# An attention and state-space stage rewritten: scores in pairs, decay sums brought by DMA, softmax's inverse applied last

## The chip, the cores and the metric

The kernel runs on one core of a Trainium2 chip. The core has a matrix engine (PE, with PEld for its weight loads), three engines for elementwise work (DVE, ACT, POOL), a queue engine for transfers (SP) and an accumulator memory, PSUM, of 8 banks with 512 float32 columns each. The metric is the time on the device in microseconds (us); less is better.

## The reference, cut to what matters

One encoder layer over two sequences of 256 and 512 tokens: a joint input projection, attention and a state-space mixer side by side, an output projection with a layer norm, a mixture of 16 experts, a last layer norm. Batch is 1 and the width 1024. The changed stage computes this:

```python
# attention: 8 query heads and 2 key heads of 64, in blocks of 128 queries
sc = jnp.einsum("bqkgd,bskd->bkgqs", q_blk * hd ** -0.5, k)
pr = jax.nn.softmax(sc, axis=-1)
o  = jnp.einsum("bkgqs,bskd->bqkgd", pr, v)
# state space: chunks of 128 tokens, 2 groups of 4 heads, a forward and a backward scan
seg = a_cum[..., :, None] - a_cum[..., None, :]
decay_in = jnp.exp(jnp.where(lower, seg, -jnp.inf))
cb = jnp.einsum("bclgn,bcsgn->bgcls", cc, bc)
y_diag = jnp.einsum("bgcls,bgrcls,bcsgrp->bclgrp", cb, decay_in, x)     # x = xs * dt
y_off  = jnp.einsum("bclgn,cbgrpn,bgrcl->bclgrp", cc, prev, jnp.exp(a_cum))
y = y_fwd + y_bwd + d_skip * xs          # then times silu(z), and a norm by group
```

## The kernel before, in words

The 768 tokens are 6 tiles of 128 (`NT = 6`): tiles 0 and 1 are the first sequence, 2 to 5 the second. Each engine runs its own program, written out in order, and semaphores connect them; so the order of the code is the order of the work, and a waiting instruction holds everything behind it on its engine.

The stages are: layer norm and the projections of q, k, v, z, x, B and C; the states that enter each chunk (`chunk_state`, PE with DVE and POOL) while q and k are turned so that the head dimension lies on the partitions (`qk_turn`); then the loop of attention and state space; then the output projection `out_proj`, a per-layer gate, the router and the experts, whose weights SP streams in.

The loop goes over 48 attention units (a tile and a head) and 12 state-space groups (a tile and one of 2 groups), four units to a group, that is 12 turns. In a unit PE computes the scores of 128 queries against all 256 or 512 keys (`scores`, L1642, full float32 with k padded by zeros for the other key head), DVE takes their maximum (`row_max`, L1209), ACT the exponential with its sum (L858), DVE the reciprocal, POOL or ACT divides (`normalise`, L620, or L892), PE turns the 2 or 4 blocks (`turn`, L1656), DVE copies them out (`pt_out`, L1218), and for four units together PE multiplies by the values (`pv`, L1665). For a state-space group PE makes the running sums of the decays in PSUM by 16 products of the steps with a triangular matrix (`decay`, L1680), ACT subtracts and takes the exponential (`decays`, L871 and L875), PE makes the product of C and B (`cb`, L1690), DVE weights the decays with it (`weights`, L1241), POOL adds the two directions (L628), and PE multiplies by x (`y`, L1707). The part that enters from outside the chunk is `before` on PE (L1699). PSUM banks: scores 0 to 2, turned probabilities 3, values 4, sums 5 and 6, `cb` and `y` 7.

What sets the order around the loop: PE waits for all turned q and k and all states ahead of it; SP issues the loads of the output projection's weights behind the last input projection (`load_wout(2, 0)`) and behind the last `before`; the output projection waits for the last attention output, the last y, and the split of its weights into a high and a low half by ACT and DVE. The experts' first weight loads wait for the output projection (`s_o`), the next for the gate (`s_pg`).

## Time and profile before

| quantity | value |
|---|---|
| median of 3 runs | 1155.25 us (1151.55 to 1155.29) |
| the profiled execution's own time | 1152.7 us |
| its span | 1150.9 us |
| mean granted clock of PE | 0.977 |
| busy share of PE / DVE / ACT / POOL | 91% / 38% / 22% / 22% |

Busy shares are averages over stages that have different limits, so the stage of interest has to be looked at by itself. In the traces a matmul in full float32 shows as two records, one in the single-pass format (operands rounded to it, fp32r) as one; their durations overlap, and what a matmul costs in a stream is the distance from one start to the next. "128*32" in a row of PE means weights with 128 rows and 32 columns. A timeline row merges neighbours of one kind: its second number is their joint duration, with the last one's end.

### The profile page before, as it was taken

The page shows a single profiled execution, that of the slowest core. Times are in us where ns is not written, and L with a number is a line of the kernel's source. Part 1 is how long each engine was busy: PE and PEld are TensorE (multiplying, and loading weights), DVE is VectorE, ACT ScalarE, POOL GpSimd, SP SyncE. Part 2 cuts the span into 40 slices and gives each one's busy share as a digit, 9 for nine tenths or more (in the row PEclk, how much of TensorE's full clock was granted, in tenths as well). Part 3 has the DMA queues.
Part 4 walks back from the last instruction along what each step waited for, and adds up shares of the span by engine and source line. Part 5 has one row for each costly group of instructions (what it writes and reads, how often), then busy time and mean ns, then how long its engine had stood idle before and what let it go on. Part 6 is the DMA issues. An engine that isn't in the chain of part 4 may idle for free.

```text
span 1150.9 us, 18483 instructions
## 1 busy us (share of the span) xinstructions
PE 1051.5 (91%) x7713; PEld 562.8 (49%) x7713; DVE 434.2 (38%) x834; ACT 258.2 (22%) x548; POOL 250.9 (22%) x295
## 2 busy tenths in 40 slices
PE   5999787978999899898999999999999999999990
PEld 3568666655555587765643333333333333333330
DVE  5426786356777877757200111101001110010117
ACT  1143244266656631230010000000000000000004
POOL 0005995224455200000100111011111110111110
PEclk9999989989999999999999999999999999999995
DMA  9110200110000351403259999999999999999976
GB/s 329 31 42 32 74 1 1 41 70 0 1 1 1 95 189 72 184 20 128 97 215 406 388 389 406 391 390 402 388 387 390 399 395 390 395 397 388 403 269 232
DMA packets 60810, 253.96 MB, mean 221 GB/s; under 512 B 7127, under 2 KB 11095, under 8 KB 44382
## 3 DMA queue, kind: packets, MB, share of 16 engines
q1 hardware_dynamic: 52542, 234.48, 52.0%
q0 software_dynamic: 8224, 18.88, 6.4%
q8 instruction: 29, 0.48, 0.2%
q14 instruction: 15, 0.12, 0.0%
HBM read 237.62 MB, written 15.73 MB: 220 GB/s over the span
## 4 chain that ended last, share of the span: by engine, by line
PE 68%; DVE 12%; DMA 8%; POOL 6%; ACT 3%; issue 2%; SPq 0%; DVEq 0%; POOLq 0%; ACTq 0%
PE ps L1918 25%; PE ps L1927 12%; DMA ring<-in_w_e_up 5%; PE ps L1559 4%; PE ps L1665 2%; PE ps L1680 2%; PE ps L1553 2%; DMA late<-in_w_e_up 2%; PE ps L1813 1%; PE ps L1770 1%; PE ps L1771 1%; PE ps L1772 1%; PE ps L1798 1%; PE ps L1799 1%; PE ps L1800 1%
## 5 line engine op out<-in xcount | busy, mean ns | idle before, releaser
L1918 PE MATMUL ps<-late,mix 128*32 128x512 f32 x1536 | 171.1, 593 | 0.7 <-DMA late<-in_w_e_up 0.7
L1918 PE MATMUL ps<-ring,mix 128*32 128x512 f32 x1536 | 170.7, 592 | 0.9 <-DMA ring<-in_w_e_up 0.8
L1441 DVE TENSOR_TENSOR mix<-mix,ps 128x768 f32<-128x768 f32 x16 | 15.3, 954 | 324.2 <-ACT mix L1002 324.2
L1002 ACT ACTIVATE mix<-ps 128x768 f32<-128x768 f32 x16 | 13.0, 810 | 479.0 <-PE ps L1918 479.0
L1918 PEld LDWEIGHTS ps<-ring,mix 128*32 128x32 f32 x1536 | 49.7, 110 | 116.4 <-issue 112.5
L1918 PEld LDWEIGHTS ps<-late,mix 128*32 128x32 f32 x1536 | 48.1, 110 | 109.8 <-issue 107.4
L1927 PE MATMUL ps<-late,mix 128*32 128x256 f32 (+1 forms) x1024 | 86.0, 487 | 1.3 <-issue 1.3
L1927 PE MATMUL ps<-ring,mix 128*32 128x256 f32 (+1 forms) x1024 | 85.7, 486 | 0.9 <-DMA ring<-in_w_e_down 0.9
L1448 DVE TENSOR_SCALAR mix<-ps,att 128x256 f32<-128x256 f32 (+1 forms) x30 | 17.1, 614 | 143.0 <-PE ps L1927 143.0
L1927 PEld LDWEIGHTS ps<-ring,mix 128*32 128x32 f32 x1024 | 33.1, 110 | 50.0 <-issue 37.8
L690 POOL COPY idx_now<-idxT 96x1 int32 (+1 forms) x14 | 2.5, 180 | 244.3 <-PE ps L1896 244.3
L1927 PEld LDWEIGHTS ps<-late,mix 128*32 128x32 f32 x1024 | 31.9, 110 | 43.7 <-issue 31.5
L685 POOL DMA_INDIRECT acc_rows<-mix,idx_now x30 | 46.8, 1561 | 15.0 <-POOL idx_now L693 10.5
L1533 PE MATMUL ps<-xl,wh 128*128 128x512 f32 (+1 forms) x128 | 45.1, 353 | 0.0
L1559 PE MATMUL ps<-ring,xT 128*128 128x512 f32 x96 | 43.9, 612 | 1.2 <-ACT xT L734 1.2
L1642 PE MATMUL ps<-xT 128*128 128x512 f32 (+1 forms) x96 | 43.6, 539 | 1.3 <-issue 1.3
L693 POOL COPY idx_now<-idx 128x2 int32 (+1 forms) x16 | 3.0, 185 | 190.2 <-DVE mix L1448 186.9
L1798 PE MATMUL ps<-ring_r,xT_r 128*128 128x512 f32 x96 | 40.5, 422 | 1.6 <-DVE cst L1379 1.6
L858 ACT ACTIVATE ring<-ps,att 128x512 f32<-128x512 f32 (+1 forms) x48 | 29.3, 611 | 48.8 <-DVE att L1210 48.7
L1119 DVE SCALAR_TENSOR_TENSOR late<-late,cw 128x770 f32<-128x770 f32 x32 | 39.1, 1226 | 0.8
L1656 PE MATMUL ps<-cst,ring 128*128 128x128 f32 x160 | 27.3, 286 | 11.9 <-DVE late L1218 5.5
L1799 PE MATMUL ps<-late_r,xT_r 128*128 128x512 f32 x96 | 37.5, 390 | 0.0
(298 smaller groups left out, 1779.2 us busy)
## 6 DMA issues: line engine op xcount, KB each, us to landing
late<-in_w_e_gate SPq DMA_DIRECT2D x32, 1024.0 KB, 18.6
late<-in_w_e_up SPq DMA_DIRECT2D x32, 1024.0 KB, 20.6
ring<-in_w_e_gate SPq DMA_DIRECT2D x32, 1024.0 KB, 16.8
ring<-in_w_e_up SPq DMA_DIRECT2D x32, 1024.0 KB, 20.6
late<-in_w_e_down SPq DMA_DIRECT2D x16, 2048.0 KB, 22.4
ring<-in_w_e_down SPq DMA_DIRECT2D x16, 2048.0 KB, 22.4
ring<-in_w_in SPq DMA_DIRECT2D x3, 2048.0 KB, 8.9
late<-in_w_ple_gate SPq DMA_DIRECT2D x2, 2048.0 KB, 15.0
```

The costliest lines, as they stand in the source:

```text
L685: pool.indirect_dma_start(acc_parts[i], bass.IndirectOffsetOnAxis(ap=idx_now[:, 1 + i:2 + i], axis=0), ye[i], None, compute_op=ALU.add).th ...
L858: nc.scalar.activation(prob[:, u % 4, 0:L], ps[:, u % 3, 0:L], ACT.Exp, bias=att[:, 0, u:u + 1], scale=HD ** -0.5, accum_out=att[:, 1, u:u ...
L1119: ins = nc.vector.scalar_tensor_tensor(conv[:, m, :], u_pad[:, m, j:j + CW], cw[:, m, j:j + 1], conv[:, m, :], ALU.mult, ALU.add)
L1533: nc.tensor.matmul(o, w_h, xl[:, k, a * P:(a + w) * P], start=False, stop=False)
L1553: last = nc.tensor.matmul(bank[:, 0:272], lhs[k], wkv[:, k, :], start=(k == 0), stop=(k == KD - 1))
L1559: last = nc.tensor.matmul(bank, lhs[k], slotk[0][:, k, :], start=(k == 0), stop=(k == KD - 1))
L1642: nc.tensor.matmul(ps[:, u % 3, 0:n * P], qT[:, h % 4, t * P:(t + 1) * P], kz[:, h // 4, a * P:(a + n) * P], start=True, stop=True).then_i ...
L1656: last = nc.tensor.transpose(ps[:, 3, b * P:(b + 1) * P], prob[:, u % 4, b * P:(b + 1) * P], ident)
L1798: nc.tensor.matmul(o, x_h, wpg_h[h][:, k, :], start=(k == 0), stop=False)
L1799: nc.tensor.matmul(o, x_h, wpg_l[h][:, k, :], start=False, stop=False)
L1918: last = nc.tensor.matmul(ps[32 * j:32 * (j + 1), GU + g, :].rearrange("p (w c) -> p w c", w=2), xeT[:, k, 32 * g:32 * (g + 1)], gu_w[q][: ...
L1927: last = nc.tensor.matmul(ps[32 * j:32 * (j + 1), DN + i, 0:cols], src[:, k, 32 * g:32 * (g + 1)], w[:, cols * c:cols * (c + 1)], start=(k ...
```

## The change

The loop now goes over 24 pairs of units; a pair is one head of each key head. Scores are three single-pass products of high and low halves of q and k (`qh`, `ql`, `kh`, `kl`), each over 64 contraction rows for one of the two key heads, into two neighbouring banks. The maximum is taken for a pair at once. Probabilities are turned undivided; ACT copies them out, not DVE; the values are multiplied pair by pair into 64 partitions for each key head; and the inverse of the sums is spread over the output's shape by PE once a tile (`inverse_rows`), copied by ACT, and multiplied in as the output is copied. The running sums of the decays aren't made anew by PE: they are turned once, written to DRAM, and SP brings them back spread over all partitions, 512 KB for each group (`load_cum`), into two buffers. DVE subtracts and clips them with the logarithm of dt added (`exponents`), ACT takes one exponential for all, and POOL multiplies with C·B (`decayed`), which PE makes for all groups ahead of the loop. The carried part and y now share bank 6; banks 0 to 3 hold scores, 4 and 5 what is turned, 7 the values.

The diff is cut to its core; many of the removed lines are in the functions above.

```diff
-        att_units = [(t, 4 * i + j) for t in range(NT) for i in range(NKV) for j in range(4)]
+        att_units = [(t, i, j) for t in range(NT) for j in range(4) for i in range(NKV)]
         NU = len(att_units)
-        NG = NU // 4
+        NPAIR = NU // 2
+        NG = NT * GROUPS
...
+        def score_bank(p):
+            return 2 * (p % 2)
+        def turn_slot(u):
+            return u + u // 8
+        def slot_free(k):
+            t, i = (k - 2) // 9, (k - 2) % 9
+            return (s_rbc, t + 1) if i == 8 else (s_pts, 8 * t + i + 1)
...
+            sp.wait_ge(s_cro, 1)
+            sp.dma_start(cum_rows, cum_out).then_inc(s_crd, 16)
+            cum_units = cum_rows.rearrange("(t d g h) l -> t g d (h l)", t=NT, d=2, g=GROUPS)
+            def load_cum(n):
+                t, g = ssd_units[n]
+                sp.dma_start(decs[n % 2].rearrange("p d h l -> p d (h l)"),
+                             bc(cum_units[t, g])).then_inc(s_decl[n % 2], 16)
+            sp.wait_ge(s_crd, 16)
             sp.wait_ge(s_proj, len(groups))
+            load_cum(0)
             load_wout(2, 0)
+            sp.wait_ge(s_st, len(upd))
+            load_cum(1)
+            for n in range(2, NG):
+                sp.wait_ge(s_m, n - 1)
+                load_cum(n)
+            sp.wait_ge(s_sc, NU)
...
+            def decayed(n):
+                dec = decs[n % 2]
+                pool.wait_ge(s_edec, n + 1)
+                pool.wait_ge(s_cbs, n + 1)
+                ch.step(nc.gpsimd.tensor_tensor(dec, dec, cbT.unsqueeze(2).broadcast_to([P, 2, HPG, P]),
+                                                ALU.mult))
+                ch.settle()
+                if n >= 2:
+                    pool.wait_ge(s_y, n - 1)
+                nc.gpsimd.tensor_tensor(msums[n % 2], dec[:, 0], dec[:, 1], ALU.add).then_inc(s_m, 1)
...
+            for n in range(NG):
+                decayed(n)
+                if n:
+                    gate(n - 1)
+                ssd_sums(n)
+            gate(NG - 1)
...
+            def cb_out(m):
+                act.wait_ge(s_cb, m + 1)
+                if m == 0:
+                    act.wait_ge(s_conv, KC)
+                copy(cbs[:, 4 * m:4 * m + 4, :],
+                     ps[:, 4 + m % 2, :].rearrange("p (n l) -> p n l", l=P)).then_inc(s_cbc, 1)
...
+            def pt_out(u):
+                t, i, j = att_units[u]
+                n = seq_of[t][1]
+                act.wait_ge(s_pt, u + 1)
+                if u >= 8:
+                    act.wait_ge(s_pv, u // 2 - 3)
+                copy(probT(u)[:, 0:n, :],
+                     ps[:, 4 + turn_slot(u) % 2, 0:n * P].rearrange("p (b c) -> p b c", c=P)).then_inc(s_pts, 1)
+            def inverse_rows_out(t):
+                act.wait_ge(s_rb, t + 1)
+                if t:
+                    act.wait_ge(s_ao, t)
+                copy(inv_rows, ps[:, 4 + (9 * t + 8) % 2, :]).then_inc(s_rbc, 1)
+            def decays(n):
+                act.wait_ge(s_dsc, n + 1)
+                v = decs[n % 2].rearrange("p d h l -> p (d h l)")
+                nc.scalar.activation(v, v, ACT.Exp).then_inc(s_edec, 1)
...
+            for p in range(NPAIR + 1):
+                if p < NPAIR:
+                    probabilities(2 * p)
+                    probabilities(2 * p + 1)
+                if p % 4 == 1 and p >= 5:
+                    inverse_rows_out((p - 5) // 4)
+                if p:
+                    pt_out(2 * p - 2)
+                    pt_out(2 * p - 1)
+                if p % 2 == 0 and p < NPAIR:
+                    decays(p // 2)
+                if p % 2 and p >= 5:
+                    squares((p - 5) // 2)
...
+            def qk_low(t):
+                dve.wait_ge(s_qkh, t + 1)
+                b = 2 * ((U_QK + t) % 2)
+                tc = slice(t * P, (t + 1) * P)
+                nc.vector.scalar_tensor_tensor(ql(t), ps[:, b, :], HD ** -0.5, qh[:, t, :], ALU.mult, ALU.subtract)
+                nc.vector.tensor_tensor(kl[:, tc], ps[:, b + 1, 0:P], kh[:, tc], ALU.subtract).then_inc(s_qkT, 1)
...
+            def row_max(p):
+                L = seq_of[att_units[2 * p][0]][1] * P
+                b = score_bank(p)
+                dve.wait_ge(s_sc, 2 * p + 2)
+                nc.vector.reduce_max(att[:, 0, 2 * p:2 * p + 2], ps[:, b:b + 2, 0:L], X,
+                                     negate=True).then_inc(s_max, 1)
+            def inverse_sums(t):
+                dve.wait_ge(s_exp, 8 * t + 8)
+                nc.vector.reciprocal(att[:, 2, 8 * t:8 * t + 8], att[:, 1, 8 * t:8 * t + 8]).then_inc(s_rcp, 1)
+            def att_out(t):
+                dve.wait_ge(s_pv, 4 * t + 4)
+                dve.wait_ge(s_rbc, t + 1)
+                nc.vector.tensor_tensor(mix[:, t, 0:512], ps[:, 7, :], inv_rows, ALU.mult).then_inc(s_ao, 1)
...
+            def exponents(n):
                 t, g = ssd_units[n]
...
+                dve.wait_ge(s_decl[n % 2], 16 * (n // 2 + 1))
                 for d in range(2):
                     for h in range(HPG):
                         c = d * NH + g * HPG + h
...
+                        v = decs[n % 2][:, d, h]
+                        last = nc.vector.tensor_scalar(v, v, d16(CSUB)[:, t, c:c + 1], d16(LDT)[:, t, c:c + 1],
+                                                       ALU.add, ALU.min)
+                last.then_inc(s_dsc, 1)
...
+            for p in range(NPAIR + 2):
+                if p < NPAIR:
+                    row_max(p)
+                if p % 4 == 0 and p:
+                    inverse_sums(p // 4 - 1)
+                if p % 2 and p < NPAIR:
+                    carried(p // 2)
+                if p % 2 == 0 and p >= 4:
+                    y_out(p // 2 - 2)
+                if p % 2 == 0 and p < NPAIR:
+                    exponents(p // 2)
+                if p % 4 == 1 and p >= 5:
+                    att_out((p - 5) // 4)
...
-            def scores(u):
-                t, h = att_units[u]
+            def scores(p):
+                t, _, j = att_units[2 * p]
                 a, n = seq_of[t]
-                if u >= 3:
-                    pe.wait_ge(s_exp, u - 2)
-                nc.tensor.matmul(ps[:, u % 3, 0:n * P], qT[:, h % 4, t * P:(t + 1) * P],
-                                 kz[:, h // 4, a * P:(a + n) * P], start=True, stop=True).then_inc(s_sc, 1)
+                if p >= 2:
+                    pe.wait_ge(s_exp, 2 * p - 2)
+                b = score_bank(p)
+                jc = slice(j * P, (j + 1) * P)
+                for step, (q, k) in enumerate(((qh[:, t, jc], kh), (qh[:, t, jc], kl), (ql(t)[:, jc], kh))):
+                    for i in range(NKV):
+                        rows = slice(i * HD, (i + 1) * HD)
+                        last = nc.tensor.matmul(ps[:, b + i, 0:n * P], q[rows], k[rows, a * P:(a + n) * P],
+                                                start=(step == 0), stop=(step == 2))
+                        if step == 2:
+                            last.then_inc(s_sc, 1)
...
+            def pv(p):
+                t, _, j = att_units[2 * p]
+                a, n = seq_of[t]
+                pe.wait_ge(s_pts, 2 * p + 2)
+                if j == 0 and t:
+                    pe.wait_ge(s_ao, t)
                 for b in range(n):
...
+                    for i in range(NKV):
+                        rows = slice(i * HD, (i + 1) * HD)
+                        last = nc.tensor.matmul(ps[rows, 7, j * P:(j + 1) * P],
+                                                kvd[:, a + b, P + i * HD:P + (i + 1) * HD],
+                                                probT(2 * p + i)[:, b, :], start=(b == 0), stop=(b == n - 1))
                 last.then_inc(s_pv, 1)
...
+            def inverse_rows(t):
+                k = 9 * t + 8
+                pe.wait_ge(s_rcp, t + 1)
+                pe.wait_ge(*slot_free(k))
+                for j in range(4):
+                    for i in range(NKV):
+                        u = 8 * t + 2 * j + i
+                        last = nc.tensor.matmul(ps[i * HD:(i + 1) * HD, 4 + k % 2, j * P:(j + 1) * P],
+                                                att[:, 2, u:u + 1].broadcast_to([P, HD]), ident,
+                                                start=True, stop=True)
+                last.then_inc(s_rb, 1)
...
             def y(n):
                 t, g = ssd_units[n]
                 pe.wait_ge(s_m, n + 1)
+                pe.wait_ge(s_offm, min(n + 2, NG))
+                if n:
+                    pe.wait_ge(s_yo, n)
...
+            for p in range(NPAIR + 2):
+                if p < NPAIR:
+                    scores(p)
+                if p >= 2:
+                    pv(p - 2)
+                if p % 4 == 1 and p >= 5:
+                    inverse_rows((p - 5) // 4)
+                if 1 <= p <= NPAIR:
+                    turn(2 * p - 2)
+                    turn(2 * p - 1)
+                if p % 2 == 0 and p < NPAIR:
+                    before(p // 2)
+                if p % 2 and p >= 3:
+                    y((p - 3) // 2)
```

On PE, a piece of the loop before, in the long turns (`xT` holds q and k, `ring` the probabilities and states, `late` here x, B and C, `gb_in` turned probabilities, `kvd` the values); 16 decay products of 128x128 stand ahead of it and behind it:

```order
L1656 MATMUL ps<-cst,ring 128x128 x4
L1642 MATMUL ps<-xT 128x512
L1690 MATMUL ps<-late 128x128
L1656 MATMUL ps<-cst,ring 128x128 x4
L1642 MATMUL ps<-xT 128x512
L1656 MATMUL ps<-cst,ring 128x128 x4
L1699 MATMUL ps<-ring,late 128x256 x2
L1665 MATMUL ps<-gb_in,kvd 128x512 x4
L1642 MATMUL ps<-xT 128x512
L1707 MATMUL ps<-late,ring 128x64 x4
```

And the like piece of the changed kernel, two pairs:

```order
L1758 MATMUL ps<-gb_in,kvd 64x128 x8
L1745 MATMUL ps<-cst,ring 128x128 x8
L1784 MATMUL ps<-ring,late 128x256
L1733 MATMUL ps<-kh,qh 128x512 x2
L1733 MATMUL ps<-kl,qh 128x512 x2
L1733 MATMUL ps<-kh,ql_53 128x512 x2
L1758 MATMUL ps<-gb_in,kvd 64x128 x8
L1770 MATMUL ps<-cst,att 64x128 x8
L1745 MATMUL ps<-cst,ring 128x128 x8
L1795 MATMUL ps<-late 128x64 x4
```

The decay products and C·B are gone from the loop; scores, values and the spread inverse are in small tiles, between turns and y in full ones.

On DVE, before, one unit's rows and the state-space part of a turn:

```order
L1209 TENSOR_REDUCE att<-ps 128x1
L1210 TENSOR_SCALAR att<-att 128x1
L1311 RECIPROCAL att<-att 128x1
L1218 COPY late<-ps 128x4x128
L1233 TENSOR_TENSOR late<-ps,cst 128x256
L1241 SCALAR_TENSOR_TENSOR ring<-ring,dtw,late 128x128 x8
L1252 TENSOR_TENSOR ring<-ps,dtw 128x256 x2
```

And in the changed kernel, a pair and the state-space part that follows it:

```order
L1281 TENSOR_REDUCE att<-ps 128x2
L1317 TENSOR_TENSOR ring<-ps,dtw 128x256 x2
L1281 TENSOR_REDUCE att<-ps 128x2
L1286 RECIPROCAL att<-att 128x8
L1327 TENSOR_TENSOR late<-late,ps 128x256
L1300 TENSOR_SCALAR ring<-ring,dtw 128x128 x8
L1305 TENSOR_TENSOR late<-late,cst 128x256
```

The y sum (L1327), which releases POOL's gate and sums, now stands right ahead of the eight scalars and the mask.

## Rows read from the trace of the kernel before

**Rows 1.** the table of windows: us from A to B, busy of each engine, PEclk, DMA share, GB/s.

```profile
281.00:388.00 107.00, 98.35 (x475) 62.04 (x476) 81.74 (x233) 66.10 (x177) 53.77 (x53) 1.00 0.01 3
596.00:1150.00 554.00, 522.09 (x5276) 185.35 (x5268) 68.31 (x106) 38.86 (x73) 68.92 (x76) 0.98 1.00 380
```

**Rows 2.** timeline of PE, turn from 333 to 347 us: start, us, line, operation, count.

```profile
333.40 1.00 PE L1707 MATMUL ps<-late,ring 128*128 128x64 f32 x8
334.21 1.98 PE L1680 MATMUL ps<-tri_r,a_r 128*128 128x128 f32 x16
336.04 0.62 PE L1656 MATMUL ps<-cst,ring 128*128 128x128 f32 x4
336.49 1.02 PE L1642 MATMUL ps<-xT 128*128 128x512 f32 x2
341.86 1.03 PE L1699 MATMUL ps<-ring,late 128*128 128x256 f32 x4
342.73 3.60 PE L1665 MATMUL ps<-gb_in,kvd 128*128 128x512 f32 x8
347.02 1.00 PE L1707 MATMUL ps<-late,ring 128*128 128x64 f32 x8
```

**Rows 3.** timeline of PE: where the loop, its long turns, its end and the next stage start.

```profile
235.14 0.67 PE L1642 MATMUL ps<-xT 128*128 128x256 f32 x2 [1.34 <-issue]
281.76 1.98 PE L1680 MATMUL ps<-tri_r,a_r 128*128 128x128 f32 x16
388.45 1.00 PE L1707 MATMUL ps<-late,ring 128*128 128x64 f32 x8
398.68 0.50 PE L1770 MATMUL ps<-ring_r,xT_r 128*128 128x512 f32 x1 [0.35 <-DVE mix L1224]
```

**Rows 4.** instructions by source line: duration ns min/median/max, first and last start, forms.

```profile
L1209 DVE TENSOR_REDUCE att<-ps x48: 404/678/694, 235.9 to 388.1; 128x1 f32<-128x512 f32 x32, 128x1 f32<-128x256 f32 x16
L1241 DVE SCALAR_TENSOR_TENSOR ring<-ring,dtw,late x96: 343/347/353, 241.6 to 386.2; 128x128 f32<-128x128 f32 x96
L1054 DVE TENSOR_SCALAR xa<-xa,mv,sd x12: 811/812/815, 6.3 to 479.9; 128x1024 f32<-128x1024 f32 x12
L858 ACT ACTIVATE ring<-ps,att x48: 455/679/689, 236.5 to 389.0; 128x512 f32<-128x512 f32 x32, 128x256 f32<-128x256 f32 x16
L628 POOL TENSOR_TENSOR ring<-ring x12: 1261/1262/1269, 243.9 to 386.6; 128x512 f32<-128x512 f32 x12
L636 POOL TENSOR_TENSOR late<-late,ring x16: 722/724/732, 245.8 to 388.7; 128x256 f32<-128x256 f32 x16
```

**Rows 5.** timeline of POOL and DVE from 386.6 us.

```profile
386.62 1.27 POOL L628 TENSOR_TENSOR ring<-ring 128x512 f32<-128x512 f32 x1 [3.49 <-DVE ring L1241]
386.78 1.39 DVE L1277 SCALAR_TENSOR_TENSOR mix<-mix,gss,ssdw 128x256 f32<-128x256 f32 x1
389.53 0.47 DVE L1277 SCALAR_TENSOR_TENSOR mix<-mix,gss,ssdw 128x256 f32<-128x256 f32 x1
```

**Rows 6.** table of windows of 5 us: PEclk is the granted clock.

```profile
240.00:245.00 5.00, 1.49 (x6) 0.80 (x6) 3.69 (x16) 2.64 (x9) 1.09 (x1) 0.94 0.00 0
245.00:250.00 5.00, 4.78 (x23) 4.78 (x23) 0.63 (x4) 1.24 (x5) 2.37 (x4) 0.50 0.00 0
365.00:370.00 5.00, 3.50 (x16) 1.92 (x16) 4.93 (x14) 3.45 (x10) 2.46 (x2) 1.00 0.01 3
405.00:410.00 5.00, 5.00 (x23) 4.13 (x22) 5.00 (x6) 2.49 (x5) 0.00 (x0) 1.00 1.04 403
```

**Rows 7.** timeline of PE in the expert stage, one change of product.

```profile
699.62 1.04 PE L1918 MATMUL ps<-ring,mix 128*32 128x512 f32 x8
700.59 1.13 PE L1896 MATMUL ps<-cst,mix 96*128 96x96 f32 x8
701.65 5.37 PE L1927 MATMUL ps<-late,mix 128*32 128x256 f32 x64
```

**Rows 8.** DMA issues by tile: count, KB each, median us from issue to landing.

```profile
gb_in<-in_ln_in_g SPq DMA_DIRECT2D x1, 512.0 KB, 5.7
```

More of the change, by code:

```diff
@@ L846, in _ @@
                 b = 2 * (u % 2)
[L847 to L851 removed]
+                nc.scalar.activation(qh[:, t, :], ps[:, b, :], ACT.Copy, scale=HD ** -0.5)
+                copy(kh[:, t * P:(t + 1) * P], ps[:, b + 1, 0:P]).then_inc(s_qkh, 1)
@@ L1221, in att_out @@
[L1221 to L1236 removed]
+                if n > len(upd) // 2 and n % 2:
+                    qk_low((n - len(upd) // 2) // 2)
@@ L1620, in _, with cb @@
                         chunk_state(n)
+            def cb(m):
+                pe.wait_ge(s_projo, len(groups))
+                if m == 2:
+                    pe.wait_ge(s_cbc, 1)
+                for n in range(4 * m, 4 * m + 4):
+                    t, g = ssd_units[n]
+                    cc = conv_col(t)
+                    last = nc.tensor.matmul(ps[:, 4 + m % 2, (n % 4) * P:(n % 4 + 1) * P], conv[:, 4 + g, cc:cc + P],
+                                            conv[:, 6 + g, cc:cc + P], start=True, stop=True)
+                last.then_inc(s_cb, 1)
             def qk_turn(t):
@@ L1686, in cb, with before @@
+            def before(n):
                 t, g = ssd_units[n]
```

314 lines of the change are left out of this document (107 added, 207 removed).

## The prediction

> **What bounds the kernel now.** I read three views in this order: the table of windows, to find the stage that the change rewrites and what is busy in it; the timeline of PE through that stage, to get the length of one turn of its loop; the groups by source line, for the price of one operation on each engine. In the windows [rows 1] the reader is to see that from 281 to 388 us PE is busy 98.35 of 107 us while DVE has 81.7, ACT 66.1 and POOL 53.8: this stage goes by PE. In the last window the DMA queues have share 1.00 for 554 us: the experts stream their weights at full rate, and that stream starts when the stages before it are done. Its first loads wait for the output projection and its other ones for the gates, so whatever the attention stage saves arrives earlier at the same stream and is kept one for one.
>
> The loop has 12 turns, one for each token tile and state-space group, with 4 heads' attention in each. Turns 0 to 3 belong to the sequence of 256 tokens, 4 to 11 to that of 512. PE's first scores start at 235.14, the long turns at 281.76, and the last y product at 388.45 [rows 3]: 153.3 us, 11.7 for a short turn (46.6 / 4) and 13.3 for a long one (106.7 / 8). One long turn in full [rows 2] runs from 333.40 to 347.02, 13.6 us. PE's part of it: y 0.81; decays 1.83; four groups of turned probabilities at 0.46, 1.83; four scores, each two records of 0.43, 3.44; two state products 0.87; values 3.43; C·B 0.4. That is 12.6, so waits take about 0.8.
>
> **The change, part by part, for a long turn.** Durations are from one profiled execution of 1152.7 us (span 1150.9 plus 1.8 around it); the median of the timed runs is 1155.25, from 1151.55 to 1155.29.
>
> PE loses the 16 decay matmuls (1.83; DMA now spreads the sums in time) and the C·B product (0.4, made ahead of the loop). Turns, state products and y stay: 1.83 + 0.87 + 0.81 = 3.5. Scores become 12 single-pass matmuls over half the contraction rows. PE does 23 of the full-width kind in 5 us [rows 6], 0.22 each: 2.6 one after another, 1.3 if the two halves of the rows run side by side. Values become 16 products with 64 output partitions and 128 columns, two records each; a record of a quarter of 0.43 is 0.107, so 3.4 in sequence and 1.7 if the two halves of the output partitions go together. The spread inverse costs 8 such records for a turn, 0.9 or 0.45. The trace shows no half tiles. It shows quarter ones: 8 records of an expert product with 32 weight columns lie within 0.97 us [rows 7], though one of 512 columns in full width takes 0.43. So I take side by side for both, and the sequence as the other bound.
>
> PE changes the shape of its tile some 6.5 times in a turn. The nearest rows are the expert's transposes between tiled products: 8 of them take 1.06 us from their start to the next product's start [rows 7], where 8 at the 0.11 of [rows 2] would take 0.9. That is some 0.07 for one change. The other bound is what a group of four transposes lasts (0.62) beyond its spacing (0.45) [rows 2], 0.17, if each shape waits for the last one to be through. I take 0.15, nearer to that, since in the loop each group is short: 1.0 us. Sum for PE: 3.5 + 1.3 + 1.7 + 0.45 + 1.0 = 8.0; in sequence 3.5 + 2.6 + 3.4 + 0.9 + 1.0 = 11.4. The Trainium skill ("TensorEngine Tiling (Array Packing)", Key Properties) says that changing the tiling mode drains TensorE and that different tiles may run in parallel; the rows agree with the second for columns, and no row shows it for contraction rows.
>
> DVE loses the copies of turned probabilities, the negation and single reciprocals. Its maximum goes over two banks at once: 678 ns for 512 columns and 404 for 256 [rows 4] give 1.07 ns a column, so 1.23, twice, 2.5. Eight weighted products (347 ns each, 2.2 for all eight) become eight two-operation scalars of 128 columns; 1024 columns of such an instruction take 812 ns [rows 4], so 128 lie between 0.15 and the 0.27 of today's spacing; 0.2, so 1.6. With C·B masked 0.4, carried part 0.75, y sum 0.4, half an output 0.34: 6.0. ACT: four exponentials with their sums at 0.68 spacing (2.7), four copies out at a little less each (2.5, from DVE), one exponential of 1024 columns for the decays (679 ns for 512 and 455 for 256 [rows 4], so 1.1), half an inverse copy 0.3, squares 0.5: 7.1; before it had eight small activations more. POOL gives up its normalising (1.5 each) and takes the product with C·B: 1.26 for 512 and 0.72 for 256 [rows 4] is 2.1 ns a column, 2.34 for 1024; then 1.26, 0.6, 1.5, 0.7: 6.4.
>
> So no engine alone has over 8 us. But DVE and POOL get in each other's way. At 386.78 a DVE product of two SBUF operands takes 1.39 us, beside a POOL sum that began at 386.62 and ended at 387.89 [rows 5]; the same instruction 2.7 us later takes 0.47 us. It was held till POOL was done. In today's loop POOL mostly waits for DVE's eight products, so they don't meet; in the new one POOL's gate and sums are released by the y sum right ahead of DVE's eight scalars. If these and the mask never run beside a POOL instruction, the two need 6.4 + 1.6 + 0.4 = 8.4 together, and behind the eight scalars stand the next maximum and all that follows it. I take 10.0 for a long turn: 8.4, and 1.6 for waits between four engines that are all near it (twice the 0.8 of today). A short turn has one carried sum fewer: 7.7, with waits 8.7; PE has 5 there. The Trainium skill ("SBUF — State Buffer", Who interferes with whom) says that DVE in a two-port mode, or with two SBUF inputs, and GpSimd block each other for a whole instruction, and that tensor_scalar has such a mode. That rule speaks against this change; the row agrees for two SBUF inputs. With it the turn is 10.0, without it 8.8.
>
> Sum of the loop: 4 x 8.7 + 8 x 10.0 = 115, against 153.3: 38 less.
>
> Ahead of the loop PE gets 12 C·B products (about 3 us, some of it in its waits), and DVE the low halves of q and k, 6 x (0.67 + 0.28) = 5.7 (the 0.67 and 0.28 by the prices of PSUM reads in [rows 4]), in a stretch in which it steps with PE. Bounds 0 and 9, all hidden or none; I take 4. The new loads of the sums, 512 KB each, land in about 6 us, as the row of that size says [rows 8]. A buffer's circle is load 6, eight scalars 1.6, ACT 3, POOL 3.6, so 14 for two turns: hidden under 2 x 8.7. From landings of 9 or 10 on it shows.
>
> The tail from the last scores to the first output projection at 398.68 [rows 3] has the same members (values, y, copies, weight halves): 0, bounds -3 and +3. 1152.7 - 38 + 4 = 1118.7, so **1119**; the median stands 0.2% over the profiled run, which I leave in the range.
>
> **Rivals.** (A) DVE and POOL hardly meet, and PE sets the pace with half tiles in parallel: 8.0 + 0.8 a long turn, 7 a short one: 98, so 1152.7 - 55 + 4 = 1102. For it: each engine's own work is under 8. Against: the row at 386.78.
>
> (B) The halves do not overlap on PE: 11.4 + 0.8 = 12.2 a long turn, 8.7 a short one: 132, so 1152.7 - 21 + 4 = 1136. For it: no row shows contraction halves together. Against: the quarter tiles.
>
> (C) Slower: PE, no longer full, is given the lower clock. At 240 to 245 us PE is busy 1.49 of 5 us, and from 245 to 250 its granted clock is 0.50, 1.2 GHz for 2.4 [rows 6]. The streaming parts then double: 15.0 + 0.8 long, 10 short: 166, +13 and +4: 1170. It decides when this clock holds for about two thirds of the loop: 115 + 51 x 0.67 = 149, which with the 4 ahead is 153. Against: from 365 to 370, with PE busy 3.50 of 5, it keeps 1.00 [rows 6].
>
> (D) The change doesn't carry: the loads of the sums or a handshake through bank 6, which the carried part and y now share, hold each turn at today's length: 153 + 4, so 1157 at most, and about 1150 if short turns gain. Bank 6 makes y wait for DVE's carried part of the next turn, which stands behind a maximum; PE has turned probabilities to do meanwhile (0.9 + 1.7 against 1.2 + 0.75), so I expect under 0.5.
>
> **How the numbers follow.** Forecast 0.48 (1108 to 1129), A 0.20, B 0.20, C 0.06, D 0.06. Below 1096 lies 0.06 of A, above 1144 all of C and D and 0.02 of B: range 1096 to 1144. A measurement of this kernel tells 0.5% (6 us) from no change. Faster: all of the forecast, A and B, 0.88. C is slower; D ends within 0.5% with 0.04 and beyond with 0.02: same 0.04, slower 0.08.
>
> **What would show it.** Right: PE's first scores near 239, its share of the loop down to some 80%, turns of 10 and 8.7 us; single scalars on DVE stretched to over 1 us where a POOL instruction runs; score records of two halves starting within 0.05 us of each other in pairs. Wrong: pairs 0.22 apart (B); scalars all at 0.15 to 0.3 (A); a granted clock of 0.50 over most windows of the loop (C); PE or DVE waiting for the DMA of the sums, or long waits before y (D). A last window that isn't as long as today's 554 us would break the step that the gain is kept.

## The result, and the profile after

The changed kernel takes 1137.81 us (median of 4 runs, 1137.32 to 1143.67) beside 1155.27 for the kernel before: ratio 0.9868, 95% interval 0.9848 to 0.9888. The forecast was 1119. The move of 17.5 us has the forecast sign, but is half of the 36 that were forecast. The profiled run took 1138.14, span 1135.6.

The engines' row of the page after, and its windows (in front of the loop, the loop, the experts); the columns are those of [rows 1]:

```profile
PE 1021.4 (90%) x7906; PEld 555.2 (49%) x7906; DVE 414.1 (36%) x678; ACT 241.2 (21%) x468; POOL 247.1 (22%) x283
```

```profile
core 0: us, PE busy (x) PEld busy (x) DVE busy (x) ACT busy (x) POOL busy (x), PEclk, DMA share, GB/s
225.00:245.00 20.00, 12.59 (x75) 10.29 (x73) 12.38 (x31) 7.74 (x17) 2.08 (x3) 0.84 0.60 157
245.00:375.00 130.00, 106.06 (x856) 81.00 (x856) 91.41 (x183) 76.76 (x191) 71.10 (x64) 0.84 0.21 66
580.00:1135.00 555.00, 521.70 (x5272) 185.09 (x5261) 68.30 (x106) 38.85 (x73) 68.73 (x76) 0.98 0.99 379
```

PE is no longer full in the loop (82% of 130 us, where [rows 1] had 92%), no other engine is either, and the granted clock is 0.84. The experts' window, moved ahead with the stream, holds the same work (PE busy 521.7 us where [rows 1] had 522.1) and still runs at the rate of the DMA: what is saved ahead of it arrives.

The marks of [rows 3], looked up in the timeline of PE after, give the whole balance:

| part | before | after | difference | forecast |
|---|---|---|---|---|
| start to first scores | 235.14 | 244.92 | +9.8 | +4 |
| first scores to last y | 153.3 | 127.0 | -26.3 | -38 |
| last y to end of span | 762.4 | 763.7 | +1.2 | 0 |
| span | 1150.9 | 1135.6 | -15.3 | -34 |

Two steps failed: the loop by 12 us and the lead-in by 6. The first shows in PE's timeline of one and a half long turns (start, time from first start to last end, operation; in brackets the idle time ahead of it and what ended it), the stretch that answers to [rows 2]:

```profile
335.81 0.50 PE L1733 MATMUL ps<-kh,qh 64*128 64x512 f32 x2
336.14 0.40 PE L1733 MATMUL ps<-kl,qh 64*128 64x512 f32 x2
336.38 0.40 PE L1733 MATMUL ps<-kh,ql 64*128 64x512 f32 x2
336.70 1.09 PE L1758 MATMUL ps<-late,kvd 128*64 128x128 f32 x16
337.73 1.09 PE L1745 MATMUL ps<-cst,ring 128*128 128x128 f32 x8
339.52 1.08 PE L1795 MATMUL ps<-late,ring 128*128 128x64 f32 x8 [0.70 <-issue]
...
345.29 1.09 PE L1758 MATMUL ps<-gb_in,kvd 128*64 128x128 f32 x16 [0.41 <-ACT gb_in L781]
346.22 1.04 PE L1770 MATMUL ps<-cst,att 128*64 128x128 f32 x16
347.19 0.65 PE L1745 MATMUL ps<-cst,ring 128*128 128x128 f32 x4
350.71 0.63 PE L1745 MATMUL ps<-cst,ring 128*128 128x128 f32 x4 [2.87 <-ACT qksq L781]
351.18 1.22 PE L1795 MATMUL ps<-late 128*128 128x64 f32 x6
```

The spread of the inverse sums (L1770) is done at 347.2, and the second group of turned probabilities needs its bank. That bank comes free only when ACT has copied the spread, and ACT's timeline shows what stands ahead of that copy:

```profile
347.09 1.06 ACT L935 ACTIVATE ring<-ring 128x1024 f32<-128x1024 f32 x1 [1.85 <-DVE ring L1300]
348.64 0.69 ACT L914 ACTIVATE ring<-ps,att 128x512 f32<-128x512 f32 x1 [0.48 <-DVE att L1281]
...
349.31 0.68 ACT L914 ACTIVATE ring<-ps,att 128x512 f32<-128x512 f32 x1
...
349.98 0.59 ACT L781 ACTIVATE qksq<-ps 128x512 f32<-128x512 f32 x1
```

The decays, then both exponentials of the new pair, then the copy. The list of waits in the loop adds these up, and says what else the engines wait for (us in total, times, longest):

```profile
DVE att L1281 <- PE ps L1733: 24.6, 11, 3.7
...
PE ps L1745 <- ACT qksq L781: 12.5, 5, 2.9
...
ACT ring L935 <- DVE ring L1300: 10.3, 6, 2.5
ACT late L935 <- DVE late L1300: 10.3, 6, 3.0
```

12.5 us in five waits. Behind the last four of them the granted clock is lower: 0.66, 0.70, 0.57 and 0.64 in the windows of 5 us from 285, 305, 330 and 350, with 1.00 from 335 to 340 between. Behind the first, at 266.9, it stays at 1.00. The lower clock also comes without such a wait: 0.50 from 365 to 370, behind waits of only 0.66 and 1.00. At the lower of the two levels (1.2 GHz for 2.4) the 16 value products at 331.70 last 1.97 us, those at 336.70 last 1.09.

A second wait stands ahead of y in each turn without a spread, and it is the handshake through bank 6. The profile calls most of it "issue", which means that it saw no releaser:

```profile
PE ps L1795 <- issue: 5.0, 5, 2.1
...
PE ps L1795 <- DVE ring L1317: 1.3, 1, 1.3
```

By the code y waits for POOL's sum of its own group, for DVE's last y sum, and for DVE's carried part (L1317) of the next group. For the y at 339.52, shown above, these two rows tell which came last:

```profile
327.52 1.27 POOL L673 TENSOR_TENSOR ring<-ring 128x512 f32<-128x512 f32 x1
...
338.68 0.74 DVE L1317 TENSOR_TENSOR ring<-ps,dtw 128x256 f32<-128x256 f32 x2
```

POOL was done at 328.79, DVE's y sum at 333.40, the carried part at 339.42, 0.1 us before y starts. All six waits, 6.3 us together, end 0.10 to 0.14 us behind the carried part, which stands on DVE behind the eight scalars, the mask and a maximum.

The collision of DVE and POOL that the prediction feared is there. DVE and POOL, the same stretch; the eight scalars (L1300) take 3.98 us beside POOL's gate and sums (3.4 to 4.0 over the long turns):

```profile
319.66 0.37 DVE L1327 TENSOR_TENSOR late<-late,ps 128x256 f32<-128x256 f32 x1
319.95 3.98 DVE L1300 TENSOR_SCALAR ring<-ring,dtw 128x128 f32<-128x128 f32 x8
```

```profile
320.11 0.76 POOL L693 TENSOR_TENSOR mix<-late,mix 128x256 f32<-128x256 f32 x1 [1.09 <-DVE late L1327]
320.83 0.61 POOL L681 TENSOR_TENSOR late<-late,hpar 128x256 f32<-128x256 f32 x1
321.52 1.55 POOL L684 TENSOR_TENSOR late<-late,ring 128x256 f32<-128x256 f32 x2
```

At 246.68, with POOL idle, the same eight take 2.13. Beside three POOL instructions of 256 columns, as at 298.58, they take 3.42, beside four 3.98: each costs the scalars 0.4 to 0.5 us, less than the 0.6 to 0.8 that it lasts. A single scalar lasts at most 0.90 us there; one of 1.88 stands in the group of 250.59, which takes 5.62 beside POOL's product with C·B.

Ahead of the loop DVE makes a low half (L1250) between two state updates and waits for a q that ACT hasn't copied; PE's state products (L1679) then wait for DVE. First DVE, then PE:

```profile
230.53 0.69 DVE L1250 SCALAR_TENSOR_TENSOR ql<-ps,qh 128x512 fp32r<-128x512 f32 x1 [2.56 <-ACT kh L781]
...
235.24 0.69 DVE L1250 SCALAR_TENSOR_TENSOR ql<-ps,qh 128x512 fp32r<-128x512 f32 x1 [1.91 <-ACT kh L781]
```

```profile
232.35 0.67 PE L1679 MATMUL ps<-qksq,late 128*128 128x256 f32 x2 [2.16 <-DVE ring L1270]
237.06 0.67 PE L1679 MATMUL ps<-qksq,late 128*128 128x256 f32 x2 [2.17 <-DVE ring L1270]
...
244.92 0.58 PE L1733 MATMUL ps<-kh,qh 64*128 64x256 f32 x2 [1.82 <-issue]
```

### The profile page after: what moved, and what is told of

Its sections match the earlier page's. It is cut to its first block, busy times and chain, and to the rows that moved or that the text cites. A ratio compares the mean times of both kernels' runs of the same rounds, so it can differ in the third digit from the quotient of the medians.

```text
span 1135.6 us, 18623 instructions
## 1 busy us (share of the span) xinstructions
PE 1021.4 (90%) x7906; PEld 555.2 (49%) x7906; DVE 414.1 (36%) x678; ACT 241.2 (21%) x468; POOL 247.1 (22%) x283
## 4 chain that ended last, share of the span: by engine, by line
PE 67%; DVE 13%; DMA 8%; POOL 5%; ACT 3%; issue 3%; SPq 0%; ACTq 0%; DVEq 0%; POOLq 0%
PE ps L2003 25%; PE ps L2012 12%; DMA ring<-in_w_e_up 5%; PE ps L1626 4%; PE ps L1620 2%; DVE ring L1300 2%; DMA late<-in_w_e_up 2%; PE ps L1854 2%; PE ps L1897 2%; DVE late L1178 1%; PE ps L1856 1%; PE ps L1855 1%; PE ps L1733 1%; PE ps L1882 1%; PE ps L1883 1%
## 5 line engine op out<-in xcount | busy, mean ns | idle before, releaser
L1508 DVE TENSOR_TENSOR mix<-mix,ps 128x768 f32<-128x768 f32 x16 | 15.3, 954 | 324.2 <-ACT mix L1061 324.2
L1745 PE MATMUL ps<-cst,ring 128*128 128x128 f32 x160 | 27.8, 316 | 12.5 <-ACT qksq L781 12.5
L1884 PE MATMUL ps<-ring_r,mix_r 128*128 128x512 f32 x96 | 37.4, 390 | 0.0
```

The lines of the kernel that those rows point to most:

```text
L1745: last = nc.tensor.transpose(ps[:, 4 + k % 2, b * P:(b + 1) * P], prob[:, u % 4, b * P:(b + 1) * P], ident)
L1884: nc.tensor.matmul(o, x_l, wpg_h[h][:, k, :], start=False, stop=False)
```

## The experiments

"Loop" below is first scores to last y in the profiled run, 127.0 for the changed kernel. The kernels e1 to e4 and e8, e11 are the changed kernel with one edit; e5 has two edits; e6 and e7 stand on e5, e9, e10 and e12 on e6. Loops, clocks and waits are each read from one profiled execution; the timed runs of one kernel lie up to 9 us apart, so a loop is told from another only to a few us.

**e1: the inverse's copy ahead of the exponentials.**

```
 for p in range(NPAIR + 1):              # ScalarE
+    if p % 4 == 1 and p >= 5:
+        inverse_rows_out((p - 5) // 4)
     if p < NPAIR:
         probabilities(2 * p); probabilities(2 * p + 1)
-    if p % 4 == 1 and p >= 5:
-        inverse_rows_out((p - 5) // 4)
```

> ScalarE copies the rows of the inverse sums before the two exponentials of the new pair, and not behind them, twice in the loop of pairs (and once where no exponentials follow). Theory (the copy's place costs TensorE three waits of 2.1 to 2.9 us and, with them, the full clock for the rest of each turn): the waits at 266.9, 327.5 and 350.7 of the trace after shrink to under 1 us, the mean granted clock of the loop rises from 0.84 to 0.90 or more, and the time falls by 6 to 12 us against the changed kernel, to 1126 to 1132. Rival (the exponentials come later by the copy, and the next pair's scores, whose banks they free, wait as long): the time moves by under 3 us, 1135 to 1141, and the waits turn up before the scores.

Measured: 1125.83 (1122.70 to 1126.50), ratio 0.9739, 0.9723 to 0.9755. 12.0 us less than the changed kernel, the theory's upper end; loop 112.3; clock 0.91. The copy moves in five turns, not in two as the expectation says, and two of the five waits stay at 1.2 us, above the 1 that was expected. In the list of waits of e1 the row is now:

```profile
PE ps L1745 <- ACT qksq L781: 4.4, 5, 1.2
```

One reordering on an engine that is 59% busy is worth two thirds of what the whole change had brought. The waits ahead of y stay, 8.1 us in five, and behind the one of 1.84 us at 329.81 the clock falls to 0.66 here too.

**e2: the scalars ahead of y.**

```
 # VectorE, even p
+exponents(p // 2)
 if p >= 4: y_out(p // 2 - 2)
-exponents(p // 2)
```

> VectorE makes the eight scalar products of the exponents before it gates y, so that they don't run beside GpSimd's gate. Theory (the two engines hinder one another: eight took 3.98 us beside GpSimd and 2.13 alone, and ScalarE's decay waits for them): the eight take 2.2 us or less in every even turn, the even turns get shorter by 1 to 1.8 us each, and the time falls by 6 to 12 us, to 1126 to 1132. Rival (the gate of y then runs beside GpSimd's other tiles and is late by as much, or GpSimd's are not what the turn ends on): the scalars get shorter, the turns don't, and the time stays within 3 us of 1137.8.

Measured: 1144.36 (1143.37 to 1145.09), ratio 0.9901, 0.9886 to 0.9917: 6.5 us more. The scalars did come down to 2.1, but y sums up in bank 6, which PE wants for the next product with the states; those now wait for it:

```profile
DVE att L1281 <- PE ps L1733: 44.9, 20, 3.7
...
PE ps L1784 <- DVE late L1327: 22.8, 10, 3.3
```

Both theories failed: a new wait, of 22.8 us, took the place of the collision. In the order as it stands the shared bank costs the 6.3 us of waits ahead of y and none of these; here it is the other way round (0.7 ahead of y for DVE).

**e3: low halves a slot later.**

```
-if n > len(upd) // 2 and n % 2:         # VectorE
-    qk_low((n - len(upd) // 2) // 2)
+if n > len(upd) // 2 + 2 and n % 2:
+    qk_low((n - len(upd) // 2) // 2 - 1)
-if t == 0: cb_out(2)                    # ScalarE
+if t == 1: cb_out(2)
```

> Ahead of the loop VectorE takes each low half of q one slot later, and ScalarE takes the third bank of cb after the second q and not after the first. Theory (the 7.6 us that the lead-in gained between 225 and 245 come of VectorE standing at a low half for a q that ScalarE has not yet, so that the states' products, and TensorE behind them, wait 2.16 us twice): the first scores start at 240 or 241 instead of 244.9, and the time falls by 4 to 6 us, to 1132 to 1134. Rival (the last low halves, now after the states, hold the first scores back by as much): first scores at 244 to 246, the time within 2 us of 1137.8.

Measured: 1131.51 (1129.69 to 1134.15), ratio 0.9799, 0.9782 to 0.9817; 6.3 us less, just over the 4 to 6 that were expected. First scores at 240.36, DVE's waits of 2.56 and 1.91 are gone and so are PE's of 2.16. The theory holds: over the profiled executions the first scores start at 243.1 to 246.6 in the six kernels without this edit and at 239.7 to 241.2 in the seven with it.

**e4: one half after the other.**

```
-for step, (q, k) in enumerate(...):     # scores
-    for i in range(NKV):
+for i in range(NKV):
+    for step, (q, k) in enumerate(...):
-for b in range(n):                      # values
-    for i in range(NKV):
+for i in range(NKV):
+    for b in range(n):
```

> The scores' and values' products of the two halves of the rows are written one half after the other instead of in turns; nothing else is changed. Theory (the products of the two halves run side by side when they alternate, as their steps of 0.23 to 0.24 us for two of 512 columns say): each long turn costs TensorE 0.6 to 0.7 us more in the scores and about 0.9 us more in the values, 11.4 against 8.0 at most, so 1 to 3 us more for each of eight pairs, 1148 to 1162. Rival (the halves already run one after the other, the records only overlap; case B of the prediction): no change, 1136 to 1140.

Measured: 1137.27 (1131.98 to 1140.98), ratio 0.9832, 0.9812 to 0.9853: no more than the changed kernel. By the time alone the rival would have won. The timeline of PE says otherwise:

```profile
337.54 0.51 PE L1733 MATMUL ps<-kh,qh 64*128 64x512 f32 x2
337.87 0.40 PE L1733 MATMUL ps<-kl,qh 64*128 64x512 f32 x2
338.10 0.41 PE L1733 MATMUL ps<-kh,ql 64*128 64x512 f32 x2
338.44 1.58 PE L1758 MATMUL ps<-late,kvd 128*64 128x128 f32 x16
339.95 1.09 PE L1745 MATMUL ps<-cst,ring 128*128 128x128 f32 x8
```

The scores still start in pairs of the two halves, 0.23 apart, though three of the one half are now written ahead of three of the other; two of 512 columns in the time that one full-width product takes ([rows 6]). PE took them out of the order in which they were written. The values, eight of a half behind each other, take 1.51 to the next start in place of 1.03. So the halves do run side by side; PE lost 0.5 us in a pair of heads and the time did not rise. A part went into PE's waits, those ahead of y fell from 6.3 to 3.2 us, and the clock was 0.88 for 0.84; how much each gave isn't parted.

**e5: e1 and e3 together** (both edits above).

> The two edits that each won time, together: the inverse's copy ahead of the exponentials, and the low halves of q a slot later. Theory (the one removes waits inside the loop of pairs, the other waits ahead of it, and nothing links them): the gains of 12.0 and 6.3 us add up, 1119.5, with the first scores at 240.4 and the first output product some 119 us later at 359.7. Rival (the tail takes part of it back, for example a transfer of weights that would be late now): over 1123.

Measured: 1121.29 (1119.13 to 1126.27), ratio 0.9709, 0.9695 to 0.9722. Of the 18.3 us 16.5 are there; with runs from 1119 to 1126 they add up, and this is the forecast's 1119 within 0.2%. First scores (239.7 for 239) and loop (114.8 for 115) are the forecast's too, but partly by luck: the loop still holds 9.8 us of waits ahead of y, which the prediction put at under 0.5 each.

**e6: e5, and y ahead of the maximum.**

```
+if p % 2 == 0 and p >= 4:               # VectorE
+    y_out(p // 2 - 2)
 if p < NPAIR:
     row_max(p)
 ...
-if p % 2 == 0 and p >= 4:
-    y_out(p // 2 - 2)
```

> The two edits of the run before, and VectorE adds y up (the bank's read) before it takes the row maxima of the new pair, so that GpSimd's gate and sums start a maximum earlier and VectorE's eight scalars begin when GpSimd is nearly through. Theory (the 3.98 us of the eight come from GpSimd's work beside them): the eight take 2.2 to 3.2 us, ScalarE's decay starts earlier, and the time falls by 3 to 7 us against the kernel with both edits, to 1113 to 1117. Rival (the maximum is what the pair waits for, and putting 0.4 us ahead of it costs each even turn that much, while the exponents were not on the path): no change or up to 3 us more, 1119 to 1123.

Measured: 1113.43 (1112.78 to 1114.92), ratio 0.9646, 0.9633 to 0.9659; 7.9 us less than e5; loop 106.4. The time is the theory's, the reason at most in part: over the last seven long turns the eight scalars take 3.3 on average for 3.7. The waits up to 355 tell more. DVE's wait for scores had 21.3 in e5, and PE's waits ahead of y had 9.8 in the whole loop; in e6

```profile
DVE att L1281 <- PE ps L1733: 4.8, 10, 0.6
...
PE ps L1795 <- issue: 3.2, 4, 1.1
```

With 0.4 at the first y that is 3.6 ahead of y, 6.2 less, of a loop that is 8.3 shorter. DVE takes the y sum while it would have waited for scores, POOL's gate starts a maximum earlier, and the carried part that the next y waits for comes earlier. That it is this order and not POOL's earlier start was not tried apart.

**e7: e5, GpSimd's gate and sums on a few columns.**

```
-tensor_tensor(z, ysum, z, mult)
+tensor_tensor(z[:, 0:8], ysum[:, 0:8], z[:, 0:8], mult)
-tensor_tensor(yadd, yadd, offm[:, d, :], add)
+tensor_tensor(yadd[:, 0:8], yadd[:, 0:8], offm[:, d, 0:8], add)
 # and the product with the skip weights on 4 columns
```

> The two edits that won time, and GpSimd's gate and its three sums of each unit work on 4 or 8 columns in place of 256: the rest of y is left as it is, so this part of the result is left out, the waits and signals are all kept. The decays' 1024 columns are not touched. It prices GpSimd's work beside VectorE's scalars. Theory: the eight scalars take 2.1 us in place of 3.98 in every pair of the loop, and the time falls by 6 to 10 us against the kernel with both edits, to 1109 to 1114. Rival (the scalars are not on the path, TensorE and ScalarE set the turn): the scalars shrink, the time by under 2 us.

Measured: 1104.65 (1102.27 to 1106.80), ratio 0.9559, 0.9542 to 0.9575: 16.6 us less than e5; loop 100.2 for 114.8. Scalars and GpSimd in one long turn:

```profile
318.45 2.14 DVE L1300 TENSOR_SCALAR ring<-ring,dtw 128x128 f32<-128x128 f32 x8
```

```profile
318.62 0.24 POOL L693 TENSOR_TENSOR mix<-late,mix 128x8 f32<-128x8 f32 x1 [1.07 <-DVE late L1327]
318.82 0.29 POOL L681 TENSOR_TENSOR late<-late,hpar 128x4 f32<-128x4 f32 x1
```

The 16.6 us are above the 6 to 10 that were expected. The waits ahead of y are down to 1.0 us from 9.8. So DVE's scalars and POOL's work beside them are on the path. The price holds both what DVE no longer loses (1.3 to 1.8 a turn) and what POOL no longer does (up to 1.9 a turn), which this kernel can't part.

**e8 and e11: the spread written five and three times**, so that PE works while it waits.

```
-for j in range(4):                      # inverse_rows
+for j in 5 * (0, 1, 2, 3):              # e11: 3 * (0, 1, 2, 3)
     for i in range(NKV):
```

> The changed kernel, but TensorE writes the spread of the inverse sums five times over the same bank before it signals, 2.1 us more work at full clock, so that it is busy for most of the 2.1 to 2.9 us in which it waits for ScalarE (all four spreads get it, the last one off this wait). It parts the price of the wait from the price of the clock that falls behind it. Theory (the clock falls because of the wait, and that costs as much as the wait): the granted clock of the loop rises from 0.84 to 0.88 or more, and the time falls by 2 to 5 us against the changed kernel, 1133 to 1136, in spite of the added work. Rival (the clock falls for another reason, or the later steps hide it): no gain, or up to 3 us more, 1137 to 1141.

Measured: 1143.81 (1142.15 to 1145.40), ratio 0.9909, 0.9894 to 0.9924; 6.0 us more. The mean clock rose to 0.91, but the four rounds more take 3.5 us (80 records in 4.54), not 2.1 as expected, so ACT came and had to wait (11.7 us for the spread, where it waited 3.7). There are six spreads, not four. The turns without a spread hint at the clock's share: y to y 9.65 us at 331.45 to 341.10, where the changed kernel has 11.1, and 9.65 at 309.31 to 318.96 for 10.3.

> The changed kernel with each of its six spreads written three times, about 1.9 us more work and not 3.5 as with five, so that it should end before ScalarE comes for it. Theory (the wait itself is the price, and the clock behind it adds to it: with five the turns between spreads took 9.7 in place of 11.1, which the added work took back): 3 to 6 us less than the changed kernel, 1132 to 1135, clock of the loop 0.88 or more. Rival (the wait alone is the price, the turns end on GpSimd's and ScalarE's chain in any case): 1136 to 1140.

Measured: 1133.46 (1132.45 to 1137.59), ratio 0.9828, 0.9808 to 0.9848; 4.4 us less than the changed kernel, with more work. The windows of the loop, of e11 and then of e1:

```profile
245.00:375.00 130.00, 107.59 (x1048) 84.28 (x1049) 95.34 (x187) 82.15 (x197) 71.52 (x64) 0.92 0.26 80
```

```profile
245.00:375.00 130.00, 106.47 (x898) 81.60 (x897) 103.83 (x196) 86.00 (x201) 71.49 (x64) 0.91 0.32 105
```

The loop takes 121.5 with the wait filled, 112.3 with it removed and 127.0 as it is. So of the 14.7 us that the wait costs, some 5 are the clock that falls behind it: 5.5 by the loops, 4.4 by the medians, and e11 has the added work in it. The rest is taken to be the wait itself, which went from 12.5 us to 4.4 in e1.

**e9, e10, e12: the lead-in's table and the wait ahead of the output projection.** e9 takes the logarithm behind the last silu:

```
-activation(dtw[:, LDT, :], dtw[:, LDT, :], Ln)   # between exp and silu
+activation(dtw[:, LDT, :], dtw[:, LDT, :], Ln)   # ahead of cb_out(0)
```

> On the kernel with three edits (copy of the inverse first, low halves later, y before the maximum): the logarithm of the step widths, for which ScalarE loads a third table at 193.2 between two others, is taken behind the last silu of the projections, and VectorE's subtraction that needs it just ahead of the loop of pairs. Theory (the extra load, 1.28 us, and the 0.28 of the logarithm stand on the path there: the trace after runs 1.6 us late from 198 on): 1.3 to 1.7 us less, 1111.7 to 1112.1, all of it seen at TensorE's products near 207. Rival (the same load stands on the path wherever it is, at the low halves too): the products near 207 come 1.6 us earlier and the first scores don't, 1113 to 1114.

Measured: 1113.12 (1111.44 to 1115.12), ratio 0.9639, 0.9625 to 0.9653: nothing against e6. Both theories failed, since PE's products near 207 didn't come earlier (209.2, where e10, with the logarithm in its old place, has 208.9). What is late there is PE's turn of the running sums (L1663), which the change put into its row and which waits for DVE, 0.4 to 1.2 us in every kernel that has it, here in the changed one:

```profile
192.54 0.32 PE L1663 MATMUL ps<-cst,dtw 128*96 128x128 f32 x1 [0.83 <-DVE dtw L1237]
```

That is about 1.1 us of the 2.2 by which PE runs late at 207. The other 1.1 is there ahead of it; kernels with the same code up to there differ by as much (1.6 late in e6, 2.8 in e10), so it stays open.

e10 repeats four turns ahead of the output projection:

```
-for j in range(4):                      # mix_turn(t)
+for j in (16 if t == 1 else 1) * (0, 1, 2, 3):
```

> On the kernel with three edits: ahead of the output product TensorE repeats the second tile's four turns fifteen times over (about 4 us of work within the 5.0 us in which it waits for VectorE's split of the weights), before it signals them. Theory (the first nine or ten steps of the output product run 0.43 apart and not 0.23 because the wait let the clock fall): they run 0.23 apart, and the time falls by 1.5 to 2 us, to 1111.4 to 1111.9. Rival (the signal of the second tile is late for ScalarE, or the clock falls all the same): no change, 1113 to 1114.

Measured: 1110.08 (1109.41 to 1113.65), ratio 0.9622, 0.9605 to 0.9639.

> The kernel with three edits, the late logarithm and the turns that fill the wait ahead of the output product, together. Theory (each removes its own delay): the gains add up, 3 to 3.7 us less than with three edits, 1109.7 to 1110.4. Rival (one of the two is worth nothing): 1111.5 to 1112.5; neither: 1113.4.

Measured: 1112.52 (1109.44 to 1114.79), ratio 0.9628, 0.9612 to 0.9644. In e6 and e10 the first products of the projection are

```profile
353.08 0.77 PE L1854 MATMUL ps<-ring_r,xT_r 128*128 128x512 f32 x1 [4.98 <-DVE ring_r L1358]
353.64 0.63 PE L1855 MATMUL ps<-ring_r,xT_r 128*128 128x512 f32 x1
```

```profile
348.84 7.59 PE L1811 MATMUL ps<-cst,mix 128*128 128x128 f32 x68
356.19 0.48 PE L1854 MATMUL ps<-ring_r,xT_r 128*128 128x512 f32 x1
356.51 0.40 PE L1855 MATMUL ps<-ring_r,xT_r 128*128 128x512 f32 x1
```

With the wait filled they run 0.23 apart from the start, without it 0.43 for nine steps, 1.8 us; but the filling took 7.6 us and not 4, so they begin 8.3 behind the last y in place of 7.0. That leaves 0.5 us, below what can be told here. e10's 3 us less are not repeated by e12, which has the same filling, so neither edit, nor both together, is shown to be worth anything. e6, e9, e10 and e12 are one level, 1110 to 1113, 3.5 to 3.8% below the kernel before.

## Why the prediction was half right

- **The turn, 10.0 and 8.7** is the step that failed most, by its term for waits: 1.6, taken as "twice the 0.8 of today", with nothing for a handshake of the spread and under 0.5 for bank 6. Measured, y to y: 9.35 short (4) and 11.2 long (the six from the fifth y to the eleventh). In place of the 1.6 stood two handshakes: 12.5 us in five waits for ACT's copy of the spread, and 6.3 in six for DVE's carried part ahead of y. With the copy moved (e1) the turn is 8.5 and 10.0, about the forecast's own numbers. The prediction counted what the spread costs PE and ACT to do, 0.45 and 0.3, and never asked what stands ahead of it on ACT's queue. e1 removes 14.7 us of loop by that alone, more than the 12 that were missing.
- **The lower clock** (C) was a rival with two thirds of the loop. It came in some windows, most of them behind waits, loop mean 0.84. Its part is some 5 us for a mean of 0.92 in its place (e11), where C had priced 51 for a whole loop at the lower level. What the lower windows that are left cost wasn't tried.
- **PE's 8.0** holds: the turn from 339.52 to 351.18, at full clock, is 8.4 us without its waits of 0.41 and 2.87, and it has a whole spread where the sum has half. Halves run side by side, in scores and values, as taken (pairs 0.23 apart; 16 value products in 1.03). A change of shape costs less than the 0.15 taken: 0.32 from the last scores to the first value product where a step is 0.23. Rival B is refuted by the records of the changed kernel and of e4, though its 1136 is the number nearest to the result: the right time for a wrong reason.
- **DVE and POOL**: the collision came, on dearer scalars and short of full exclusion. Eight scalars alone are 2.13, not 1.6 (the upper bound of 0.27 each was right); with POOL 3.4 to 4.0; the sign named for it, single scalars over 1 us, came only once (1.88). The 8.4 as a sum of times that exclude each other isn't what the trace shows: POOL's 2.35 and 1.28 run while DVE mostly reads PSUM, and the scalars lose 1.3 to 1.9 a turn. e7 shows that this pair is on the path; with both shortened the kernel nearly reaches rival A's 1102 (1104.65). The Trainium skill ("SBUF — State Buffer", Who interferes with whom) has the one that comes second blocked for the whole instruction. The trace agrees that the scalars are held, but by 1.85 us beside 2.92 of POOL's records (3.98 for 2.13), so not for all of the time that those show.
- **ACT's and POOL's prices** were right: 1.06 for the decays (1.1), 2.35 for 1024 columns (2.34), and so was DVE's maximum, 1.22 (1.23).
- **Lead-in +4** was +9.8, above the upper bound of 9. C·B cost its 3 us. The low halves cost 4.6 of wait that e3 removes by their order, not by their work; the bounds counted work only. The turn of the sums is about 1 more, and about 1 is open (e9).
- **Loads and bank 6** (D): the sums land in 3.4 to 4.2 us (6 taken) and nobody waits. Bank 6 costs 0.56 to 2.12 us in six turns, where under 0.5 was expected, since not only a maximum but the eight stretched scalars stand ahead of the carried part. The same bank has 22.8 us of waits in e2's order. D as a whole was wrong: the turns did get shorter.
- **The tail, 0 with 3 either way**: +1.2, from parts that nearly cancel. The kernel before still has attention behind its last y, the changed one has none: the output projection starts 7.0 behind the last y for 10.2. It then reaches the per-layer gate 3.2 later: seven steps at the lower clock (1.4), turns inside it that stood ahead of it before (0.9 net), waits of 1.5 and 0.5 at L1931, against a wait of 1.65 at 403.34 that the kernel before had there. 1.2 more are lost behind that, cause open. Gains ahead were kept nearly one for one: from last y to the end the span has 763.7 us in the changed kernel and 764.8 in e1.

## What to carry to other kernels

When a change puts a small step between two engines (here one product and one copy a tile), price the place in each queue, not the step: what stands ahead of the copy, which buffer it holds, and who wants that next. When no engine is full any more, PE's cost says little (e4 took 0.5 us more a pair and no more time), and moving single steps within their queues is worth as much as the change itself: e1, e3 and e6 together bring 24 us where the change brought 17.5. A wait that the profile calls "issue" has a cause too: list what the code waits for there and see which of them ended last. Look at the sign of the time and at the records separately: here a wrong mechanism (B) had the best number.

## What the runs showed of the hardware

- Products on half of the contraction rows ran in pairs even when three of one half were written ahead of three of the other (e4), while sixteen short ones written in two blocks of eight took 1.51 us in place of 1.03.
- A DVE instruction with a scalar pointer for each partition, both operands in SBUF, 128 columns: eight take 2.13 us with POOL idle (2.13 to 2.25 beside POOL instructions of 4 and 8 columns, e7), 3.42 beside three POOL instructions of 256 columns and 3.98 beside four. DVE's maximum, which reads PSUM, takes 1.21 to 1.23 everywhere, in e6 at 314.24 beside POOL's gate too.
- Four of the five waits of 2.1 to 2.9 us of PE for the spread are followed by windows at a granted clock of 0.57 to 0.70, the first is not. In e8, with the wait filled by spare work, the stretch from 325 to 340 has 1.00.
